# Splitting the normed tiles two per period, moving a kept norm product to VectorE, and the gate maxima's parts ahead of the value copies, in a two-layer hybrid block

## The reference

```python
h = rms_norm(x, norm1_g)
proj = h @ w_in                      # aq, ak, av, ao, ag, ...
qk = silu(centred_dwconv(concat(aq, ak), conv_w))     # three taps
q, k = split(qk);  k = k * 128 ** -0.5;  v = heads(av)
g = ag + gate_bias                   # i_fwd, f_fwd, i_bwd, f_bwd of 4 heads
h = mlstm_scan(q, k, v, i_fwd, log_sigmoid(f_fwd)) + flip(mlstm_scan(flip(q), ...))
# centred head norm over h, times norm_g, times sigmoid(ao)
```

## Time and profile before

| | |
|---|---|
| median of 3 runs | 3843.06 us (3841.88 to 3846.55) |
| profiled execution: span, first to last instruction | 3844.5 us |
| TensorE matmul busy | 3642.5 us (95%) |
| VectorE busy | 1980.4 us (52%) |
| ScalarE busy | 1634.2 us (43%) |
| GpSimd busy | 402.0 us (10%) |
| mean granted TensorE clock | 0.968 |
| mLSTM projection stage, layer 0 | about 1500 to 1620 us |
| the same, layer 1 | about 2663 to 2784 us |

### The profile page before, as it was taken

One profiled execution on the slowest core, in us unless ns is written; L12 is line 12 of the kernel. 1 busy time (PEld: TensorE's weight loads), 2 busy tenths in 40 slices (PEclk: granted clock), 3 DMA queues, 4 the chain that ended last, 5 costly groups with the idle time before them and its releaser, 6 DMA issues. The chain is left out here.

```text
span 3844.5 us, 52297 instructions
## 1 busy us (share of the span) xinstructions
PE 3642.5 (95%) x20532; PEld 2868.1 (75%) x20532; DVE 1980.4 (52%) x3166; ACT 1634.2 (43%) x2544; POOL 402.0 (10%) x353
## 2 busy tenths in 40 slices
PE   8898889969999999899999999999899999999998
PEld 6456777758878887677777788887687777788887
DVE  5879565584443334655545443333655545443332
ACT  5454432545333334456444433223456445433222
POOL 0027233000001111320000001100020000001100
PEclk9899889979999999999999999999999999999999
DMA  3012001203232232112212232333212212232232
GB/s 124 11 47 61 1 2 62 72 3 123 91 104 94 97 96 91 55 55 72 68 65 87 90 102 93 98 93 95 66 50 73 68 50 99 85 105 93 98 93 77
DMA packets 84161, 289.34 MB, mean 75 GB/s; under 512 B 9200, under 2 KB 9456, under 8 KB 82672
## 3 DMA queue, kind: packets, MB, share of 16 engines
q1 hardware_dynamic: 83520, 283.68, 23.1%
q10 hardware_dynamic: 432, 2.78, 0.2%
HBM read 284.32 MB, written 2.10 MB: 75 GB/s over the span
## 5 line engine op out<-in xcount | busy, mean ns | idle before, releaser
L492 DVE TENSOR_TENSOR weights_lo_r<-raw_weights,weights_hi_r 128x1024 fp32r<-128x1024 f32 (+2 forms) x554 | 637.9, 1152 | 1278.1 <-ACT weights_hi_r L486 1277.8
L486 ACT ACTIVATE weights_hi_r<-raw_weights 128x1024 fp32r<-128x1024 f32 (+2 forms) x554 | 546.7, 987 | 1263.6 <-PE ps L565 1212.5
L564 PE MATMUL ps<-xn_r,weights_hi_r 128*128 128x512 f32 x2688 | 1057.8, 394 | 0.0
L563 PE MATMUL ps<-xn_hi,weights_hi_r 128*128 128x512 f32 x1632 | 670.5, 411 | 46.1 <-DVE xn_r L558 18.3
L565 PE MATMUL ps<-xn_hi,weights_lo_r 128*128 128x512 f32 x1632 | 646.0, 396 | 0.0
L564 PEld LDWEIGHTS ps<-xn_r,weights_hi_r 128*128 128x128 f32 x2688 | 511.6, 190 | 106.1 <-issue 5.3
L563 PE MATMUL ps<-y_r,weights_hi_r 128*128 128x512 f32 x1200 | 469.6, 391 | 2.4 <-PEq L890 2.4
L565 PE MATMUL ps<-y_r,weights_lo_r 128*128 128x512 f32 x1200 | 466.9, 389 | 0.0
L563 PEld LDWEIGHTS ps<-xn_hi,weights_hi_r 128*128 128x128 f32 x1632 | 312.6, 192 | 141.7 <-issue 49.7
L565 PEld LDWEIGHTS ps<-xn_hi,weights_lo_r 128*128 128x128 f32 x1632 | 313.1, 192 | 69.0
L563 PEld LDWEIGHTS ps<-y_r,weights_hi_r 128*128 128x128 f32 x1200 | 225.2, 188 | 53.7 <-issue 6.4
(11 more groups left out here) (575 smaller groups left out, 5328.8 us busy)
## 6 DMA issues: line engine op xcount, KB each, us to landing
raw_weights<-in_w_ffn_dram SPq DMA_DIRECT2D x132, 512.0 KB, 3.7
raw_weights<-in_w_down_dram SPq DMA_DIRECT2D x48, 512.0 KB, 3.5
raw_weights<-in_w_out_dram SPq DMA_DIRECT2D x24, 512.0 KB, 3.5
raw_weights<-in_w_down_dram SPq DMA_DIRECT2D x24, 384.0 KB, 3.1
raw_weights<-in_w_hgrn_dram SPq DMA_DIRECT2D x16, 512.0 KB, 3.5
raw_weights<-in_w_mix_ssm_dram SPq DMA_DIRECT2D x16, 512.0 KB, 3.8
raw_weights<-in_w_a_qk_dram SPq DMA_DIRECT2D x16, 512.0 KB, 3.5
raw_weights<-in_w_mix_a_dram SPq DMA_DIRECT2D x16, 512.0 KB, 3.5
```

The source lines that it names most:

```text
L486: act.activation(self.k.w_hi[:, g % 2, 0:chunk.width], self.k.raw[:, slot, 0:chunk.width], ACT.Copy)\
L492: dve.tensor_tensor(self.k.w_lo[:, g % 2, 0:chunk.width], self.k.raw[:, slot, 0:chunk.width], self.k.w_hi[:, g % 2, 0:chunk.width].bitcast ...
L563: pe.matmul(out, w_hi, x_hi, start=start, stop=False)
L564: pe.matmul(out, w_hi, x_lo, start=False, stop=False)
```

## The change

Four edits, with nothing of the arithmetic changed except the order of two factors in one product.

1. `Entry` makes two normed tiles a period instead of one: tiles 2c-2 and 2c-1 in periods 1 to 4, their low parts one period later, in front of the next two tiles.
2. The normed x of the first layer is made by VectorE, one instruction a tile, in periods 9 to 12 (one tile each), 15 and 16 (two each). GpSimd does nothing there.
3. The value copies are shared: ScalarE takes two banks, VectorE the other two. This holds for both stages with `tokens`.
4. ScalarE does two sigmoids a period (periods 14 and 15), so the maxima's high part and the columns come at the head of period 16, ahead of the value copies. TensorE's turning of the rows moves behind the chunk of period 15, VectorE's low part of the maxima to the head of period 16.

```diff
+    def tiles_of(self, c):
+
+        return range(2 * c - 2, 2 * c) if 1 <= c <= self.tiles // 2 else ()
+
+    KEPT = {9: (0,), 10: (1,), 11: (2,), 12: (3,), 15: (4, 5), 16: (6, 7)}
+
     def scalar(self, act, upto):
-        c = self.turn("scalar")
-        if 1 <= c <= self.tiles:
-            act.wait_ge(self.normed, c)
-            self.src.make_hi(act, c - 1).then_inc(self.source_hi, 1)
+        for m in self.tiles_of(self.turn("scalar")):
+            act.wait_ge(self.normed, m + 1)
+            self.src.make_hi(act, m).then_inc(self.source_hi, 1)
 
     def vector(self, dve, upto):
         c = self.turn("vector")
-        if 1 <= c <= self.tiles:
+        for m in self.tiles_of(c - 1):
+            dve.wait_ge(self.source_hi, m + 1)
+            self.src.make_lo(dve, m).then_inc(self.source_ready, 1)
+        for m in self.tiles_of(c):
             dve.wait_ge(self.rstd_ready, 1)
...
-        if 2 <= c <= self.tiles + 1:
-            dve.wait_ge(self.source_hi, c - 1)
-            self.src.make_lo(dve, c - 2).then_inc(self.source_ready, 1)
-
-    def gpsimd(self, pool):
-        if not self.first:
-            return
-        pool.wait_ge(self.first_ready, 1)
-        pool.wait_ge(self.tile_used, 1 + KD)
-        for m in range(self.tiles):
-            pool.wait_ge(self.normed, m + 1)
-            pool.tensor_tensor(self.x[:, m, :], self.x[:, m, :], self.r_first, ALU.mult).then_inc(self.kept, 1)
-            pool.wait_ge(self.kept, 2 * m + 1)
-            pool.tensor_scalar(self.x[:, m, :], self.x[:, m, :], self.k.col(self.first, m), None, ALU.mult)\
-                .then_inc(self.kept, 1)
+        for m in self.KEPT.get(c, ()) if self.first else ():
+            dve.wait_ge(self.first_ready, 1)
+            dve.wait_ge(self.normed, m + 1)
+            dve.scalar_tensor_tensor(out=self.x[:, m, :], in0=self.x[:, m, :], scalar=self.k.col(self.first, m),
+                                     in1=self.r_first, op0=ALU.mult, op1=ALU.mult).then_inc(self.kept, 1)
...
+        def tokens_of(j):
+            o, taken = tokens[1][:, j], k.ps[:, (t0 + j) % 4, 0:width]
...
+            return o, taken
...
             if tok:
                 act.wait_ge(stream.chunk_used, tok.g0 + tok.per)
...
-                    act.activation(o, taken, ACT.Copy).then_inc(tokens_used, 1)
+                for j in range(NT // 2):
+                    act.activation(*tokens_of(j), ACT.Copy).then_inc(tokens_used, 1)
             list(side_pieces)
...
+            if tok:
+                dve.wait_ge(stream.chunk_used, tok.g0 + tok.per)
+                for j in range(NT // 2, NT):
+                    dve.tensor_copy(*tokens_of(j)).then_inc(tokens_used, 1)
             list(side_pieces)
...
-        for _ in range(12):
+        for _ in range(13):
             yield
         pe.wait_ge(self.rows_ready, 10)
...
             act.activation(self.o_gate[:, m, :], self.o_gate[:, m, :], ACT.Sigmoid).then_inc(self.o_ready, 1)
-            yield
+            if m % 2:
+                yield
...
+        yield
         dve.wait_ge(self.max_hi, 1)
         dve.tensor_tensor(self.maxima.lo, self.maxima.full, self.maxima.hi.bitcast(F32), ALU.subtract)\
             .then_inc(self.max_lo, 1)
```

More of the change, by code:

```diff
@@ L813, in vector @@
     def vector(self, dve, upto):
         c = self.turn("vector")
-        if 1 <= c <= self.tiles:
+        for m in self.tiles_of(c - 1):
+            dve.wait_ge(self.source_hi, m + 1)
+            self.src.make_lo(dve, m).then_inc(self.source_ready, 1)
+        for m in self.tiles_of(c):
             dve.wait_ge(self.rstd_ready, 1)
-            dve.scalar_tensor_tensor(out=self.src.full[:, c - 1, :], in0=self.x[:, c - 1, :],
-                                     scalar=self.weights[:, c - 1:c], in1=self.rstd, op0=ALU.mult, op1=ALU.mult)\
+            dve.scalar_tensor_tensor(out=self.src.full[:, m, :], in0=self.x[:, m, :],
+                                     scalar=self.weights[:, m:m + 1], in1=self.rstd, op0=ALU.mult, op1=ALU.mult)\
@@ L919, in project @@
         block = ctx.enter_context(nc.Block())
+        def tokens_of(j):
+            o, taken = tokens[1][:, j], k.ps[:, (t0 + j) % 4, 0:width]
+            if len(o.shape) == 3:
+                taken = taken.rearrange("p (h v) -> p h v", h=o.shape[1])
+            return o, taken
         @block.sync
```

## The result

The changed kernel takes 3816.72 us (median of 4 runs, 3808.32 to 3823.53); the kernel before took 3844.2 beside it (4 runs, the three above among them). The ratio is 0.9921 [0.9907, 0.9934]: faster, by 27.5 us between these medians and by 30 us (25 to 36) by the ratio. The profiled run of the changed kernel is the fastest of its four, 3808.32 us, which is 1.9 us above its span of 3806.4. If as much lay around its span of 3844.5, the profiled run of before took 3846.4, about what the slowest of its three did. Between the two traces lie 38.1 us, between the medians 27.5. Both differences need an explanation. One later run of the kernel before (9177 us) and one of the changed kernel (7240 us) took about twice as long at a full granted clock and are left out of every figure.

What follows compares the result with a forecast made beforehand. TensorE, busy 95% of the span, was taken as the bound, so its mLSTM-stage waits count. Terms 19.3 + 11.4 + 9.2 + 1.8 - 0.6 = 41.1 us off the median 3843.06 give 3802.0 us; range 3795 to 3815.

Steps and rivals of the forecast that it cites:

- three waits: TensorE's waits in each mLSTM stage: period 9's low part, the turning behind period 14, the barrier at the end.
- The entry and the turning: Two tiles a period end period 9's wait, gaining 19.3 us; turning the rows one chunk later gains 11.4 us.
- The kept x: Layer 0's normed x, moved from GpSimd to VectorE: costs nothing, or 5.9 us if not covered by idle time.
- The end of the stage: Barrier gap behind the mLSTM stage falls from 6.32 to 1.74 us, gaining 9.2 us over two layers.
- The other stage with tokens: VectorE's two copies end that stage some 0.3 us a layer later; from 0.57 gained to 0.8 lost.
- The scan's start: Scan's first unit runs at full clock behind the shorter gap: 1.8 us gained for both layers, bounds 0 and 2.
- A: Early periods give part back: TensorE waits for weight splits, 2 to 8 us a layer, 3806 to 3818 us; chance 0.16.
- B: VectorE becomes the bound in layer 0's late periods, by kept products before weight splits: 3808 to 3812 us; chance 0.06.
- C: The stage's end doesn't shrink, something else holding the barrier, or the turning still waits: 3811 to 3813 us; chance 0.07.
- D: Slower: TensorE loses full clock over chunks from period 9 on and doesn't regain it, about 3852 us; chance 0.03.

Runs made afterwards that it cites:

- pool_keeps: The changed kernel with layer 0's kept (normed) x made by GpSimd again: 3817.33 us, ratio 0.9916.
- control: The changed kernel measured again, unaltered: 3815.04 us, ratio 0.9922.
- before_fill: The kernel before with 22 extra unused matmuls behind the last chunk of each mLSTM stage: 3852.97 us, ratio 1.0014.
- fill_picks: The run fill with one more full matmul ahead of each of the four gate picks in the early periods: 3817.69 us.
- fill: The changed kernel with five extra unused matmuls behind the last chunk of the mLSTM stage: 3808.31 us, ratio 0.9898.
- fill_part: The run fill with value copies shared in the mLSTM stage alone; ScalarE makes all four in the other stage with tokens: 3816.28 us.
- unsplit: The changed kernel with all four value copies on ScalarE again in every stage: 3810.41 us, ratio 0.9906.
- u_fill9: The run unsplit with nine extra unused matmuls behind the last chunk of the mLSTM stage: 3808.19 us.
- again: The changed kernel measured once more, unaltered, in a later group: 3815.54 us, ratio 0.9918.
- u_fill4: The run unsplit with four extra unused matmuls behind the last chunk of the mLSTM stage: 3808.61 us.

## Why the prediction was right and where it was wrong

The direction and the mechanism of the gain were right: three waits in each layer, and all three went as forecast. The time was not. 3802.0 was predicted and 3816.7 measured, 1.7 us above the top of the range of 3795 to 3815. Carried over by the ratio 0.9921 to the median of 3843.06 from which the forecast started, it is 3812.7, inside the range and 10.7 above the forecast.

- **The entry and the turning**, 19.3 + 11.4 = 30.7 us: measured 19.3 + 10.9, which is 15.50 in layer 0 and 14.63 in layer 1, 30.1 together. The turning gave 0.5 less because chunks 15 and 16 with the turning between them take 12.2 us, where 11.95 were reckoned. Every chunk from 8 on follows the one before without a pause, but for the turning. But the terms aren't separable as I put them. Two tiles alone take the whole first wait away and give 3.5 us of it back at the turning in layer 0. What I counted as gain of the delay needs the kept x on VectorE too, as pool_keeps shows.
- **The kept x**, cost nothing: right as a cost, but the edit is worth 2.8 us in layer 0, with everything else in place. I had put GpSimd's effect on VectorE inside the entry's term; it is in the late periods' gate rows.
- **The end of the stage**, 9.2: measured 2 x 4.67 = 9.3. The gap was forecast at 1.74 and is 1.65; the last instructions are the two pairs of copies.
- **The other stage with tokens**, 0.3 a layer later: 0.18 in both layers. What the term left out is the clock behind that gap, another 1.6 us in layer 1 of the first trace and in both layers of control.
- **The scan's start**, a gain of 1.8 "with bounds 0 and 2": this is the step that failed. I looked whether the clock is full at the first matmul behind the gap. It is (0.46 us, as forecast). It falls after that, in the first unit, and the low stretch then lies over work. Measured against the earlier trace rows and the same three spreads in layer 1: +2.49 and -0.76 in the profiled run, so a loss of 1.7 us; +2.77 and +2.65 in control, a loss of 5.4. In control this term alone is 7.2 us off. The nearest row I took, one matmul of 0.47 us behind the other stage's gap of 2.00 us, could not tell: that matmul takes 0.47 us whether the clock falls behind it or not. before_fill shows, in the kernel before, that a gap of about the new length makes the loss; the bound below nothing was missing.

The two profiled runs then fit: 30.1 + 9.3 - 1.7 - 0.4 (the other stage's gap) = 37.3, against 37.2 from the first pick on; 0.9 more lie ahead of it, which makes the 38.1 us between the spans. That the profiled run was the fastest of its four is luck. The slower run control has another 3.20 and 1.61 us at half clock behind the picks, which the trace of before didn't have, and 1.5 and 1.4 us more behind the scans' first two units, where the other stage's gap and the clock behind it lie: 30.1 + 9.3 - 5.4 - 4.8 - 2.9 = 26.3, against 26.4 from the first pick on. It is the slowest of its six, mostly for what lies ahead of the first pick. The medians, 27.5, 30.8 and 30.8 us apart, lie between the two traces. I had drawn the sum from one trace and subtracted it from the median, as if each trace had the same low stretches. Whether the change itself makes them more frequent at the picks is open. Of ten traces with two tiles a period (fill_picks left out) nine have 39.7 us there in layer 0 and one 36.46; of three with the old entry one has 39.7. In layer 1 five of the ten are slow and none of the three. That is suggestive, and three traces are few.

Rivals A, B and C did not come: no wait for L492 in periods 3 to 8 or 10 to 16, and copies last at the barrier. B's condition, VectorE short of time in layer 0's late periods, came in pool_keeps, with GpSimd in the way. Of D there is a trace: a clock lost over work, some 10 us at the scan's start, and in control over the dense chunk behind the picks and the first matmuls of the other stage.

**A version that beats both.** Extra matmuls in the gap are the one addition that helped, if not surely. The changed kernel has 15 runs, median 3815.4 (3808.3 to 3825.8). fill and fill_part have nine, median 3809.8 (3804.4 to 3818.0). unsplit and its two fills have fourteen, median 3808.6 (3803.0 to 3817.9). The best single ones are fill (ratio 0.9898) and u_fill9 (0.99 [0.9884, 0.9916]), whose intervals overlap with the changed kernel's. From the first pick on, fill and fill_part take 7.3 us less than control and again, with the same length behind the picks (39.7 and 38.1 us), and 6.1 of it are the scans' starts. The first trace of the changed kernel, 2290.5, is lower than all of them, but it had full clock behind the picks in both layers, 4.8 us that the others mostly didn't have. So the gain of fill is shown for these traces, and the median of fill_part, 3816.28, doesn't speak against it; that it holds in every run isn't shown. unsplit, with no extra work, comes as low (2294.4), so no run shows a gain from sharing the copies. That the longer gap is the reason isn't shown for the whole time: unsplit had one of the two picks at full clock, and u_fill4, with slow scan starts, has its short time from the part ahead of the first pick.

## What to carry to other kernels

Ask of every wait that a change shortens not only whether the clock is up at its end, but where the low stretch will lie then: one that was hidden in idle time can come to lie over work. The first matmul behind a gap doesn't tell; read the granted clock over the 10 us behind it. Filling 5.0 us of a gap of 6.3 with unused work made this kernel 5.5 us slower. When runs differ by more than an edit can be worth, compare traces between the same two matmuls around the edit, not whole times. And take the terms of a sum from one trace, but the expected median from several: the low stretches of a single trace are a draw.

## What was not expected of the hardware

- The clock fell about 3 us after TensorE had stopped, though it had been back at work for over 1 us: it stopped at 1597.30, was back at 1598.94, and the grant is 0.86 in 1599.0 to 1600.5 and 0.50 from there. In all traces in which it fell ahead of the scan's second spread, it did so 2.3 to 5.1 us behind the last matmul ahead of the gap. With dense work behind a gap of 2.18 us (the other stage with tokens) the first matmul takes 0.47 us, and yet the clock falls 0.7 to 1.6 us behind the gap's end in 12 of 14 cases. The first matmul of the first trace, layer 0, one of the two cases where it doesn't:

```profile
1765.43 0.47 PE L563 MATMUL ps<-xn_hi,weights_hi_r 128*128 128x512 f32 x1 [2.18 <-PEq L888]
```

- Runs of one kernel differ by 17 us (0.45%), with no wait of TensorE different by over 1 us in the stages looked at. The Trainium skill ("TensorE: Matmul & The Clock Gate", § What's actually happening) says that the same kernel shows different counts of slow matmuls from run to run; the runs here agree, and show that for a kernel of 3.8 ms it doesn't average out.
- VectorE's instructions of 128 rows beside GpSimd's were on the mean 26% (weight split, 1532 against 1220 ns) to 126% (first tap of the convolution, 1085 against 481 ns) longer, by holds on some of them and none on others.
